# All of TensorE's unread products of the identity taken out of a two-block kernel

## The reference, cut to what matters

```python
def reference(x, norm_mix, w_in, ...):
    x = first_block(x, ...)      # h = rms_norm(x); x += hybrid_mixer(h); h = rms_norm(x); x += hier_moe(h)
    return second_block(x, ...)

# second_block, for i in range(4), mixers mlstm, swa, hgrn2, diff:
        h = x * (1 + scale[0][:, None]) + shift[0][:, None]
        ...
        x = layer_norm(DEEPNORM_ALPHA * x + (1 + gate[0][:, None]) * y.astype(x.dtype), ln_g[i, 0], ln_b[i, 0])
        h = x * (1 + scale[1][:, None]) + shift[1][:, None]
        y = swiglu(h, ffn_w_in[i], ffn_w_out[i])
        x = layer_norm(DEEPNORM_ALPHA * x + (1 + gate[1][:, None]) * y.astype(x.dtype), ln_g[i, 1], ln_b[i, 1])
```

## Time and profile before

| | us |
|---|---|
| median of 3 runs | 2415.37 (2413.93 to 2417.48) |
| profiled execution | 2420.73 |
| its span, first to last instruction | 2418.9 |
| PE busy (matmul) | 2290.5 (95%) |
| PE busy (weight load) | 1937.8 (80%) |
| DVE, ACT, POOL busy | 1822.2 (75%), 1152.4 (48%), 130.5 (5%) |
| DMA | 572.52 MB, mean 237 GB/s |

### The profile page before, as it was taken

How to read it: one execution, slowest core, us unless ns; L and a number is a source line. 1 busy time by engine, 2 the same in 40 slices (tenths; PEclk the granted TensorE clock), 3 DMA queues, 4 the chain that set the end, 5 groups by cost and what they waited for, 6 DMA issues and landing times. The chain is left out here.

```text
span 2418.9 us, 30378 instructions
## 1 busy us (share of the span) xinstructions
PE 2290.5 (95%) x12045; PEld 1937.8 (80%) x12045; DVE 1822.2 (75%) x2033; ACT 1152.4 (48%) x1197; POOL 130.5 (5%) x229
## 2 busy tenths in 40 slices
PE   7999888999999999989999999999999999898997
PEld 7889677778888888877788787887887788796886
DVE  6887676578888889856788777887676887777545
ACT  4443234367777767644344263442642444364442
POOL 2000100000000000000011000110001111000000
PEclk9999988899999999999999999999999999999999
DMA  8843552489999999954699436994623898344662
GB/s 301 272 130 120 180 171 81 117 318 370 369 355 374 355 371 358 370 176 147 201 384 357 146 123 190 384 363 142 201 94 133 266 375 311 119 142 148 191 191 70
DMA packets 347057, 572.52 MB, mean 237 GB/s; under 512 B 68128, under 2 KB 181280, under 8 KB 346912
## 3 DMA queue, kind: packets, MB, share of 16 engines
q1 hardware_dynamic: 326176, 495.02, 60.5%
q0 software_dynamic: 20736, 75.51, 8.2%
HBM read 569.39 MB, written 1.05 MB: 236 GB/s over the span
## 5 line engine op out<-in xcount | busy, mean ns | idle before, releaser
L286 DVE TENSOR_TENSOR st_lo<-st_raw,st_hi 128x2048 fp32r<-128x2048 f32 (+1 forms) x195 | 441.1, 2267 | 140.8 <-ACT st_hi L276 140.6
L276 ACT CAST st_hi<-st_raw 128x2048 fp32r<-128x2048 f32 (+1 forms) x195 | 368.3, 1893 | 251.3 <-PE ps L316 174.2
L286 DVE TENSOR_TENSOR es_lo<-es_raw,es_hi 128x2048 fp32r<-128x2048 f32 x192 | 429.2, 2285 | 76.1 <-ACT es_hi L276 74.9
L314 PE MATMUL ps<-st_hi,sb_h_hi 128*128 128x512 f32 (+1 forms) x1232 | 464.8, 377 | 14.5 <-DVE sb_h_lo L1115 7.4
L316 PE MATMUL ps<-st_hi,sb_h_lo 128*128 128x512 f32 (+1 forms) x1232 | 455.1, 369 | 0.0
L315 PE MATMUL ps<-st_lo,sb_h_hi 128*128 128x512 f32 (+1 forms) x1232 | 454.7, 369 | 0.0
L276 ACT CAST es_hi<-es_raw 128x2048 fp32r<-128x2048 f32 x192 | 357.6, 1912 | 48.2 <-PE ps L316 23.1
L314 PEld LDWEIGHTS ps<-st_hi,sb_h_hi 128*128 128x128 f32 x1232 | 235.9, 191 | 57.0 <-issue 14.6
L316 PEld LDWEIGHTS ps<-st_hi,sb_h_lo 128*128 128x128 f32 x1232 | 235.4, 191 | 39.1
L315 PEld LDWEIGHTS ps<-st_lo,sb_h_hi 128*128 128x128 f32 x1232 | 236.1, 192 | 35.7
L314 PE MATMUL ps<-es_hi,moe_hg_hi 128*128 128x512 f32 x512 | 205.7, 402 | 1.9 <-PEq L61 1.9
(11 more groups left out here) (688 smaller groups left out, 3811.8 us busy)
## 6 DMA issues: line engine op xcount, KB each, us to landing
st_raw<-in_ffn_w_in_dram SPq DMA_DIRECT2D x176, 512.0 KB, 6.5
t_aw<-in_ada_w_dram POOLq DMA_DIRECT2D x144, 512.0 KB, 7.0
es_raw<-in_w_expert_gate_dram SPq DMA_DIRECT2D x64, 1024.0 KB, 8.1
es_raw<-in_w_expert_up_dram SPq DMA_DIRECT2D x64, 1024.0 KB, 7.5
es_raw<-in_w_expert_down_dram SPq DMA_DIRECT2D x64, 1024.0 KB, 7.2
st_raw<-in_ffn_w_out_dram SPq DMA_DIRECT2D x44, 1024.0 KB, 7.6
fb_aw<-in_ada_w_dram SPq DMA_DIRECT2D x39, 512.0 KB, 6.1
hs_raw<-in_w_in_dram SPq DMA_DIRECT2D x36, 512.0 KB, 7.1
```

The lines of the kernel that those rows point to most:

```text
L276: act.copy(p.at(self.hi[:, m % self.held, :]), p.at(self.raw[:, n % self.slots, :])).then_inc(self.high, 1)
L286: dve.tensor_tensor(p.at(self.lo[:, m % self.held, :]), p.at(self.raw[:, n % self.slots, :]), p.at(self.hi[:, m % self.held, :]).bitcast(F ...
L314: pe.matmul(out, a_hi, b_hi, start=start, stop=False, skip_group_check=True)
```

## The change

The function `stir` and all its calls are removed, with the arguments `stirs` that lead to them. With the calls go the waits that stood only ahead of them: for `drained` at the end of `project`, for `biased` in `turn`, and for `placed` in `WovenHeads`. The waits for `drained` in `delta_rule` and `hgrn` stay. Nothing else is changed.

```diff
--- before.py
+++ after.py
@@ -314,12 +314,6 @@
     pe.matmul(out, a_hi, b_hi, start=start, stop=False, skip_group_check=True)
     pe.matmul(out, a_hi, b_lo, start=False, stop=False, skip_group_check=True)
     return pe.matmul(out, a_lo, b_hi, start=False, stop=stop, skip_group_check=True)
-
-
-def stir(k, pe, bank, count):
-
-    for _ in range(count):
-        pe.matmul(k.ps[:, bank, 0:P], k.ident[:], k.ident[:], start=True, stop=True)
 
 
 def weave(*parts):
@@ -459,7 +453,7 @@
     return pieces
 
 
-def project(k, name, finish, feature_major=False, also=(), beside=None, between=None, stirs=0):
+def project(k, name, finish, feature_major=False, also=(), beside=None, between=None):
 
 
 
@@ -530,10 +524,6 @@
                     if j == 0 and closes(n) and len(halves(n)) == 2:
                         last.then_inc(half, 1)
                 last.then_inc(S.used, 1)
-            if stirs:
-                for j in range(2):
-                    pe.wait_ge(drained[j], turn[j][-1])
-                stir(k, pe, 4 * (1 - turn[0][-1] % 2), stirs)
 
         def drain(eng, n, j):
             if j not in halves(n):
@@ -639,7 +629,6 @@
                     at = i % 2 * T + t * P
                     last = pe.transpose(ps[:, 4 + i // 2, at:at + P], k.X[:, t, i * P:(i + 1) * P], k.ident[:])
                 last.then_inc(turned, 1)
-            stir(k, pe, 0, 8)
             open_features(k, pe, lambda kt: (hs, splits_for(kt)))
 
         @block.scalar
@@ -892,8 +881,6 @@
         def _(pe):
             def turn_norm(site, t):
                 for i in range(8):
-                    if t and i == 0:
-                        stir(k, pe, 0, 9)
                     if i % 4 == 0:
                         pe.wait_ge(normed, 4 * site + 2 * t + i // 4 + 1)
                     at = i % 2 * T + t * P
@@ -1287,10 +1274,9 @@
             for dst, src in self.loads:
                 sp.dma_start(dst, src).then_inc(self.landed, 16)
 
-    def sums(self, pe, stirs=0):
+    def sums(self, pe):
         pe.wait_ge(self.ada.added, self.ada.total)
         for i in range(16):
-            stir(self.k, pe, 0, stirs)
             last = pe.matmul(self.psum[:, i:i + 1], self.ada.thirds[i // 8][:, i % 8 * P:(i % 8 + 1) * P],
                              self.k.ones[:, 0:1], start=True, stop=True)
         last.then_inc(self.summed, 1)
@@ -1422,7 +1408,7 @@
 
         @block.tensor
         def _(pe):
-            mod.sums(pe, 1)
+            mod.sums(pe)
             for t in range(NT):
                 pe.wait_ge(q["normed"], t + 1)
                 for i in range(8):
@@ -2440,7 +2424,6 @@
             yield 200
             for t in range(NT):
                 pe.wait_ge(gb.g.drained[t], len(gb.g.chunks))
-            stir(k, pe, 0, 24)
 
         def chain_act(act):
             after = Chain(act, q["astep"])
@@ -2753,9 +2736,6 @@
 
         def turn(pe, i):
             n, t, heads = units[i]
-            if i in (2, 12, 13, 14, 15):
-                pe.wait_ge(q["biased"], i + 1)
-                stir(k, pe, 4 + i % 3, 5)
             pe.wait_ge(q["raised"], i + 1)
             for j in range(2):
                 for kt in range(t + 1):
@@ -3253,7 +3233,7 @@
 
                 def conv_and_adds(st, drained, landed):
                     return {**short_conv(k, B, st), **adds(1, 3, 4, 5, 6, 8, 9, 10, 11)}
-                project(k, "sc_in", features_to(k, B.u), True, stirs=8, between=fetches(0, (5, 6, 7, 8, *range(10, 20))),
+                project(k, "sc_in", features_to(k, B.u), True, between=fetches(0, (5, 6, 7, 8, *range(10, 20))),
                         beside=lambda st, drained, landed: adds(*range(1, 11)),
                         also=[(B.cwa[:, j, :], column(A["conv_a_w"][0, j])) for j in range(3)])
                 def features_and_steps(eng, psum, j, n0, n1):
@@ -3558,12 +3538,12 @@
 
 
     def __init__(self, k, st, part, U, preps, rotated, units, turns, at, turn_at, lag, q_of, k_of, v_of, mask, out_of, dv,
-                 stirs, moved, depth=6, sinks=None, lam=None):
+                 moved, depth=6, sinks=None, lam=None):
         self.moved, self.depth = moved, depth
         self.k, self.S, self.part, self.U, self.preps, self.rotated = k, k.stream, part, U, preps, rotated
         self.units, self.turn_list, self.at, self.turn_at, self.lag = units, turns, at, turn_at, lag
         self.q_of, self.k_of, self.v_of, self.mask, self.out_of, self.dv = q_of, k_of, v_of, mask, out_of, dv
-        self.sinks, self.lam, self.stirs = sinks, lam, stirs
+        self.sinks, self.lam = sinks, lam
         self.first, self.end = self.S.range[part]
         self.owner = {i: u for u, turn in enumerate(turns) for i in turn[2]}
         self.sc, self.PT = st.sb("sc", [P, depth, 520]), st.sb("PT", [P, 2, 2 * BANK])
@@ -3638,9 +3618,6 @@
         out = self.k.ps[:, 6:8, :].rearrange("p b n -> p (b n)")
         for u, (t, outs, of, v) in enumerate(self.turn_list):
             yield self.mark("turn", u, self.turn_at[u])
-            if u >= len(self.turn_list) - 2:
-                pe.wait_ge(self.placed, len(self.preps))
-                stir(self.k, pe, 2, self.stirs)
             if self.lam is None:
                 pe.wait_ge(self.raised, of[-1] + 1)
             else:
@@ -3828,7 +3805,7 @@
                        v_of=lambda h, kt: U[:, kt, P + (h // 8) * D:P + (h // 8 + 1) * D],
                        mask=lambda t, n: band[:, t, :n],
                        out_of=lambda t, hs: y[:, t, hs[0] * D:(hs[-1] + 1) * D].rearrange("p (j s d) -> p s j d", s=2, d=D),
-                       dv=D, stirs=0, moved=moved, sinks=sinks)
+                       dv=D, moved=moved, sinks=sinks)
         past = PastNorm(k, st, A, 1)
         early = EarlyOut(k, st, y, w, 1, (1, 2))
         block = st.block()
@@ -3933,7 +3910,7 @@
             return {("sp", 0): lambda sp: past[0].load(sp), ("act", 1): raise_bounds, ("dve", 1): centre,
                     ("dve", 2): lambda dve: past[0].scale(dve, 0), ("dve", 3): lambda dve: past[0].scale(dve, 1),
                     ("act", 4): gates, ("act", 6): keys, ("dve", 6): running}
-        project(k, "hg_fq", features_to(k, QF), feature_major=True, also=also, beside=decays, stirs=12)
+        project(k, "hg_fq", features_to(k, QF), feature_major=True, also=also, beside=decays)
 
         with Stage(nc, "hg") as st:
             IG, aT, aX = st.sb("IG", [P, NT, 2048]), st.sb("aT", [P, NT, H, P]), st.sb("aX", [P, H, P])
@@ -4071,7 +4048,6 @@
                     v, b = LEVELS[n], 2 ** LEVELS[n]
                     if n == 1:
                         pe.wait_ge(q["first"], 1)
-                        stir(k, pe, 6, 8)
                     pe.wait_ge(q["scaled"], n + 1)
                     if n < 2:
                         pe.wait_ge(q["first"], 1)
@@ -4105,7 +4081,6 @@
                 yield 200
                 for t in range(NT):
                     pe.wait_ge(g.drained[t], len(g.chunks))
-                stir(k, pe, 0, 16)
                 for i in range(8):
                     if i % 4 == 0:
                         pe.wait_ge(q["gated"], i // 4 + 1)
@@ -4177,7 +4152,7 @@
                        v_of=lambda h, kt: U[:, kt, (3 * (h // 2) + 2) * HB + h % 2 * P:(3 * (h // 2) + 2) * HB + (h % 2 + 1) * P],
                        mask=lambda t, n: k.causal[:, t, :n],
                        out_of=lambda t, hs: y[:, t, hs[0] * P:(hs[-1] + 1) * P].rearrange("p (s j d) -> p s j d", s=1, d=P),
-                       dv=P, stirs=0, moved=moved, lam=lam[:, 0:1])
+                       dv=P, moved=moved, lam=lam[:, 0:1])
         past = PastNorm(k, st, A, 3, room=sq)
         early, scaled = EarlyOut(k, st, y, w, 3, (7, 2)), st.sem("y_scaled")
         block = st.block()
```

## The result

The changed kernel takes 2424.7 us (median of 6, 2422.01 to 2426.31), beside 2415.43 us for the kernel before on the same chip (median of 6, 2413.76 to 2417.48). The ratio is 1.0034, with a 95% interval of 1.002 to 1.0048: 8.2 us slower by the ratio (4.8 to 11.6), 9.3 by the medians. Forecast were 2428 us and slower, with 2414 to 2441 as the range. The sum of the parts was 12.3 us, above the upper end of what was measured, 11.6.

A forecast was written before the change was run, and what follows sets the result against it. TensorE was taken to set the pace of the long stretches, with losses at the joints. Terms 1.3 + 0 + 3.0 + 3.8 - 0.5 + 4.7 = 12.3 us on the median 2415.37 gave 2428 us, range 2414 to 2441.

The forecast's parts named there:

- R2: Rival, chance 0.08: stirs at router and scores are plain delay, the clock holds without them; -6 us, 2409.4 us.
- R3: Rival, chance 0.12: small work does not bring the clock back; +26 us, 2442 us.
- R1: Rival, chance 0.18: no real change, the lost clock falls into waits; +4 us, 2419 us.
- F: Seven norms of the layer tails: without their 63 stirs, work there runs at the low clock; +4.7 us (+1 to +9).
- the low level comes behind the stirs already: Four of seven norms: clock already low behind the stirs, only the eight transposes join it; +0.2 us each, +0.8.
- D: Router, 32 stirs: shorter TensorE path, but low-clock logit products and gather; +3.8 us (-2.5 to +6).
- so they take 6.8: Router: the 32 logit records, 3.66 us before, run at the low clock and take 6.8 us; +3.2 us.
- the prediction's own sign of being wrong: Router: the prediction is wrong if the logit products (L1438) stay near 3.7 us instead of near 6.8.
- C: Third mixer's first projection, 12 stirs: wait grows to 4.6 us, clock falls, 32 small fp32 records slow; +3.0 us (0 to +5.5).
- A: End of the first projection, 8 stirs: gap grows to 3.5 us and the clock falls; +1.3 us (0 to +2.3).
- E: Scores of the sparse attention, 25 stirs: path time regained against clock lost; -0.5 us (-2.5 to +2.5).
- B: Delta rule's end, third mixer's end and level 1, first features: stirs in waits, clock low behind them already; 0 (0 to +3).

The follow-up runs named there:

- e1: Only the 63 stirs at the seven norms removed from the kernel before; 2423.99 us beside 2417.16, ratio 1.0036.
- e8: All stirs removed from the kernel before except the 63 at the norms; 2419.84 us beside 2419.03, ratio 0.9998.
- e2: Only the router's 32 stirs removed from the kernel before; 2417.04 us, ratio 1.0000.
- e10: Kernel before with longer norm stirs (12 or 17 for 9, plus 6 behind and 12 ahead at some), all other stirs removed; ratio just below 1, interval including 1.
- e3: Only the 8 stirs behind the first projection and 12 behind the third mixer's first projection removed from the kernel before; 2419.95 us, ratio 1.0009.
- e6: Kernel before with each 128-column identity product at the seven norms replaced by a one-column product; 2430.38 us, ratio 1.0043.

## Why the prediction was right, step by step

**The direction and the mechanism** held at the norms: nothing in the long stretches, a lower mean clock, slower work behind the joints. R2 (faster) is out, and so is R3 (2442). R1 (2419) lies 5.7 us below the measured time; for the places other than the norms, taken together, it was right, for the norms it was not.

**F, the norms (4.7): undersized.** Measured between the same instructions 6.5 us (7.3 with the mixer behind the joint at 1377.5), timed by e1 8.7 us (5.1 to 12.3). By joints, the mean of the three kernels without against the mean of the six with: at 1175 +1.9 forecast, 1.4 measured; at 1475 +1.0 and 1.3; at 2212 +1.0 and 1.3; and at the four others, put at +0.2 each, 0.1, 1.0, 1.0 and 0.4, together 2.6 and not 0.8. That is the step that was too small ("the low level comes behind the stirs already"). With all nine stirs the joint at 1679 takes 14.96 to 16.56 us and that at 1869 20.17 to 20.87: in some executions the stirs save the clock there, in others not, and before's one profile showed mostly the latter. The joint at 2074 says least: e8, with all nine, is the slowest there (21.93).

**D, the router (3.8): mis-sized.** Timed 0.0 (-3.6 to +3.4). The step that failed is "so they take 6.8" of the 32 logit records: they take 6.88 in e2's trace and 3.92, 4.11 and 3.77 in those of the changed kernel, e8 and e10. The gather's first two products took 1.19 us instead of 0.70 in the changed kernel and e10, as low as forecast, and 0.70 in e8. So the prediction's own sign of being wrong, logit products near 3.7 us, came true here, yet R2's gain of 2.5 us did not (49.30 against 49.87 us for the stretch). The total is below what five rounds resolve.

**C, the third mixer's projection (3.0): the fall as forecast, its cost too high.** PE's timeline of the changed kernel and two windows, then one line of e8's timeline:

```profile
1742.83 5.18 PE L4043 MATMUL ps<-hg_QF,hg_K 128*128 128x128 f32 x32 [4.51 <-PEq L61]
1747.76 0.48 PE L314 MATMUL ps<-st_hi,sb_h_hi 128*128 128x512 f32 x1
```

```profile
1742.40:1745.60 3.20, 2.77 (x13) 2.80 (x14) 2.88 (x4) 2.73 (x2) 0.00 (x0) 0.50 0.79 227
1745.70:1748.00 2.30, 2.30 (x22) 2.30 (x21) 1.69 (x1) 2.27 (x2) 0.00 (x0) 1.00 0.36 134
```

```profile
1737.23 6.62 PE L4059 MATMUL ps<-hg_QF,hg_K 128*128 128x128 f32 x32 [4.51 <-PEq L61]
```

The wait grew from 1.84 to 4.51 us (4.6 forecast) and the clock fell, as said. Halfway through the products the clock was back, and they took 5.18 us, not near 7. That is one draw of several: in e3 they took 5.25 us, but in e8 and e10, also without these stirs, 6.62 and 6.76, which is the forecast. (The pace that I had taken from the 64-column products therefore was near enough for these of 128 columns at the low level.) In all eight traces with the twelve stirs they took 3.81. What was too high is the cost on the whole path: from 1741 to 1790 the four kernels without them needed 47.90, 47.98, 49.62 and 50.30 us, a mean of 48.95, and the eight with them 46.36 to 49.06, a mean of 47.63. So it is some 1.3 us and not 3.0, in a stretch that varies by 2.7 with the stirs in place. Which wait swallows the rest was not traced.

**A, the first projection (1.3): right in size where the clock falls** (+1.5, 41.31 against 39.80). The gap of 3.5 us that it rests on came about in two of the four traces without the stirs (3.16 and 3.24 us); in e3's and e10's it was 1.63 and 1.76 and cost nothing.

**E (-0.5) and B (0):** ratios of 1.0004 and 1.0007 for the two, nothing measurable, as said. In the traces E's early stirs gave back 1.0 us and the late ones nothing (26.71 to 26.65): the 1.4 us that were to come back there turned into waits for ScalarE.

**The sum.** 1.3 + 3.0 + 3.8 - 0.5 of the 12.3 were forecast for places that e8 puts near zero together, and the norms got 2 to 4 us too little. So 7.6 us were forecast where little or nothing can be measured, and the total came within some 4 us of the measured 8.2 because the norms were put too low at the same time. The range, which held, owes that in part to luck. The correction by which the time was referred to the median of the runs (the profiled execution lay 5.4 us above it) was needed. Before's trace has more time at the low level than the changed kernel's in a place with nothing removed: 111.6 to 238 has 13.7 us of it and took 126.36 us, and then 6.8 and 125.06. That is 1.3 of the 5.9 us by which the spans understate the change; the rest was not traced to places. (248.6 to 335.6 shrank too, from 87.01 to 85.70, but 1.0 of this is the early stirs of E.)

That transposes give no full clock, by which the sum would have been 15.3 ("TensorE: Matmul & The Clock Gate" of the Trainium skill, section on PE-mode transpose), is not what the traces show. In E itself the clock did fall in all four traces without its stirs, as by that sentence, but the 2.5 us that this was to cost did not appear. At the router it came back behind transposes. In the changed kernel it was low from 438:

```profile
438.00:445.00 7.00, 6.86 (x35) 6.77 (x35) 3.33 (x4) 3.42 (x6) 1.12 (x2) 0.53 0.74 127
445.50:448.50 3.00, 3.00 (x30) 3.00 (x28) 2.90 (x3) 1.31 (x2) 0.00 (x0) 1.00 1.05 401
```

In the first window PE did eight products of one column, sixteen records (such products keep no clock, e6), and sixteen transposes; in the second it is at 1.00. In e8 and e10 the clock came back behind the same work, too. The measurement decides against that sentence for this kernel's transposes. That they don't bring it back each time is e2's row.

## What to carry to other kernels

Products that nobody reads were worth something here at the norms, where a wait of some 3 us on VectorE stands ahead of a stretch in which TensorE never pauses: 63 of 196 earned all that could be measured. Elsewhere the traces show single gains (1.5 us at A when the gap was long) and a loss (1.0 us ahead of E's unit 2), which the timings can't resolve. Give such products columns, not just instructions: one-column products filled the same wait and were worth nothing. Size such an effect from several executions, since one profile shows one draw of where the clock falls.

## What the runs showed of the hardware

**One kernel's time follows its clock.** Over 35 executions of the kernel before, the time and the mean granted clock correlate at -0.94, with 19 us per 0.01 of clock (2428.82 us at 0.967, 2410.23 at 0.976). Since 0.01 of the mean is 48 us at the low level instead of the high one, 0.40 us are lost for each of them, near the 0.47 of dense work.

**Across kernels the mean clock misleads.** The changed kernel's mean clock is 0.012 lower than before's profiled execution, which at that rate would be 23 us; it lost 9.3. E8 ran at 0.965 in the time of before. Without stirs more of the low level lies in waits, where it costs nothing: E is such a place, low from 383.8 on in the changed kernel and as long as before. The mean has to be split by windows into low time with PE busy and low time with PE waiting.

**The clock can come back behind small products.** At the router it came back within or just behind the sixteen transposes in three traces (changed, e8, e10) and not in e2's. Behind C it came back 2.9 and 3.0 us into the 32 records of 128 columns in the changed kernel and e3, and 5.9 and 6.2 us into them in e8 and e10. The 32 of 64 columns stayed low to their end. So a row of one execution tells that it can happen, not that it will.
